# Second and third layers' output projections from fp32r halves, modulation sums in the value projections, and scores of two heads in turn

## What is computed

```python
    for i in range(DEPTH):                       # first_block: gMLP, then MLA, both with memory attention
        mix, q_mem = ...
        x = x + jnp.concatenate([mix, mem_out], axis=-1) @ w_out      # 256x1536 @ 1536x1024
        x = x + hierarchical_moe(rms_norm(x, norm2_g[i]), ...)        # 32 experts, all evaluated
...
    ada_in = jax.nn.silu(c)
    for i in range(DEPTH):                       # second_block
        mod = (ada_in @ w_ada[i] + b_ada[i]).reshape(b, 6, d)         # w_ada[i]: 1024 x 6144
        sh_m, sc_m, g_m = ...                    # modulation: shift, scale, gate
        hm = rmsnorm(x, norm_mix[i]) * (1 + sc_m) + sh_m
        y = dilated_mixer(hm, ...)  if i == 0 else forgetting_mixer(hm, ...)
        x = x + g_m * y                          # y ends in "@ w_out", 1024x1024
        hf = rmsnorm(x, norm_ffn[i]) * (1 + sc_f) + sh_f
        x = x + g_f * hierarchical_moe_2(hf, ...)                     # 16 experts, all evaluated
```

## Time and profile before

| | |
|---|---|
| three runs | 1508.47, 1515.75, 1517.82 us; median 1515.75 |
| the profiled execution | 1506.89 us; its span, first to last instruction, 1505.2 us |
| granted TensorE clock, mean over the span | 0.988 |
| busy: TensorE, VectorE, ScalarE, GpSimd | 94%, 49%, 33%, 7% |
| moved by DMA | 469.80 MB, 312 GB/s over the span |

### The profile page before, as it was taken

One profiled execution on the slowest core, in us unless ns is written; L12 is line 12 of the kernel. 1 busy time (PEld: TensorE's weight loads), 2 busy tenths in 40 slices (PEclk: granted clock), 3 DMA queues, 4 the chain that ended last, 5 costly groups with the idle time before them and its releaser, 6 DMA issues. The chain is left out here.

```text
span 1505.2 us, 23579 instructions
## 1 busy us (share of the span) xinstructions
PE 1412.2 (94%) x9085; PEld 770.8 (51%) x9090; DVE 737.2 (49%) x1659; ACT 495.8 (33%) x996; POOL 102.9 (7%) x258
## 2 busy tenths in 40 slices
PE   7999999998899899999779998899899998989998
PEld 4486433322375544333227876788655337755432
DVE  1368333221255545322227755675585346669534
ACT  3222121111226403111126656565612126661211
POOL 0000021110000001111102000200001102000110
PEclk9999999999999999999999999999999999999999
DMA  8996989999974269999997472335279997427996
GB/s 359 372 350 254 417 347 415 420 421 421 427 299 186 113 281 415 399 422 421 420 425 303 174 286 72 112 146 211 91 270 422 420 424 300 170 110 297 422 420 250
DMA packets 63400, 469.80 MB, mean 312 GB/s; under 512 B 7809, under 2 KB 15921, under 8 KB 18738
## 3 DMA queue, kind: packets, MB, share of 16 engines
q1 hardware_dynamic: 63282, 468.22, 76.7%
HBM read 465.42 MB, written 2.76 MB: 311 GB/s over the span
## 5 line engine op out<-in xcount | busy, mean ns | idle before, releaser
L1664 PE MATMUL PS<-ring,catT 128*32 128x512 f32 x3072 | 347.9, 594 | 12.3 <-issue 11.9
L826 PE MATMUL PS<-w_split,h_split 128*128 128x512 f32 x1152 | 270.0, 393 | 6.0 <-DVE w_split L911 6.0
L826 PEld LDWEIGHTS PS<-w_split,h_split 128*128 128x128 f32 x1152 | 213.6, 188 | 56.1 <-DVE w_split L911 8.5
L1664 PEld LDWEIGHTS PS<-ring,catT 128*32 128x32 f32 x3072 | 95.8, 110 | 228.2 <-issue 227.9
L911 DVE TENSOR_TENSOR w_split<-ring,w_split 128x512 fp32r<-128x512 f32 x192 | 133.5, 711 | 66.4 <-ACT w_split L859 66.1
L1687 PE MATMUL PS<-ring,row_place 128*32 128x512 f32 x1232 | 141.8, 593 | 14.0 <-issue 14.0
L859 ACT CAST w_split<-ring 128x512 fp32r<-128x512 f32 x192 | 118.0, 619 | 104.1 <-PE PS L826 103.6
L1874 ACT ACTIVATE row_place<-PS 128x256 f32<-128x256 f32 x48 | 18.5, 385 | 360.3 <-PE PS L1664 360.3
L508 PE MATMUL PS<-ring,catT 128*128 128x512 f32 x224 | 96.7, 592 | 1.0 <-PEq L1022 1.0
L1687 PEld LDWEIGHTS PS<-ring,row_place 128*32 128x32 f32 x1232 | 40.9, 110 | 104.9 <-issue 104.3
L1557 POOL COPY catT<-xsT 128x256 f32 x176 | 63.1, 402 | 395.0 <-PE PS L1664 387.4
(11 more groups left out here) (445 smaller groups left out, 1835.0 us busy)
## 6 DMA issues: line engine op xcount, KB each, us to landing
ring<-in_moe SPq DMA_DIRECT2D x269, 1024.0 KB, 13.8
ring<-in_w_ada SPq DMA_DIRECT2D x16, 3072.0 KB, 12.1
ring<-in_a_w_in SPq DMA_DIRECT2D x23, 2048.0 KB, 10.4
ring<-in_b_w_in SPq DMA_DIRECT2D x8, 2048.0 KB, 20.3
first_down<-in_moe SPq DMA_DIRECT2D x8, 1024.0 KB, 8.5
ring<-in_a_w_out SPq DMA_DIRECT2D x2, 3072.0 KB, 14.4
ring<-in_b_w_out SPq DMA_DIRECT2D x2, 3072.0 KB, 16.4
ring<-in_w_mem_kv SPq DMA_DIRECT2D x2, 2048.0 KB, 12.2
```

The source lines that it names most:

```text
L826: last = nc.tensor.matmul(PS[:, 2 * (i % 2) + t, :], hs[:, hp, k, t * P:(t + 1) * P], wk[:, (KT * i + k) % splits, wp, :], start=k == 0 an ...
L1664: last = nc.tensor.matmul(PS[lanes, 4 + i % 2, :].rearrange("p (g f) -> p g f", g=2), xf[:, i % 2, k, lanes], gate_up_weights(2 * i + q % ...
```

## The change

- `project_rows_split`, a new function, makes the output projections of the second and third layer from halves as `project_heads_split` does: 24 and 16 k tiles of six matmuls, room for four split k tiles, and the last three k tiles of the second column half taken row tile by row tile. It sums no modulation chunk. The fourth layer keeps `project_rows`.
- Of the 5 chunks that this frees, two go into the value jobs of each half of the third layer and one into those of the fourth (`sums`). Their places in the list of chunks move: 2 chunks (6 MB) leave the part ahead of the second expert stage, 3 (9 MB) the part ahead of the third. `project_heads_split` loads the silu row once the last mean is made.
- `scores1` of the dilated attention takes the two heads of a pair in turn, group by group.

```diff
 c_bin = weight_amid("b_w_in", 8, [512, 320, 512], [0, 1, 1])
 c_qup = weight("b_w_q_up", 4, [1536])
 c_kvup = weight("b_w_kv_up", 2, [2048])
-c_bout = weight_amid("b_w_out", 12, [512] * 2, [1, 0], 1)
+c_bout = weight("b_w_out", 12, [512] * 2)
 c_moe1 = experts("moe1", 32, ASIDE[1])
-c_ain2 = weight("a_w_in_2", 8, [512] * 18)
-c_aout2 = weight_amid("a_w_out_2", 8, [512] * 2, [1, 0], 2)
+c_ain2 = weight_amid("a_w_in_2", 8, [512] * 18, [0] * 8 + [1, 1] + [0] * 7 + [1], 1)
+c_aout2 = weight("a_w_out_2", 8, [512] * 2)
 c_moe2 = experts("moe2", 16, ASIDE[2])
-c_bin2 = weight("b_w_in_2", 8, [512] * 3 + [16] + [512] * 3)
+c_bin2 = weight_amid("b_w_in_2", 8, [512] * 3 + [16] + [512] * 3, [0] * 7, 1)
 c_bout2 = weight_amid("b_w_out_2", 8, [512] * 2, [1, 0], 2)
 c_moe3 = experts("moe3", 16, ASIDE[3])
+def ada_sum(c, m, row):
+    w = stream.view(ada_at[c], 6)
+    return nc.vector.tensor_tensor_reduce(w[:, m, :], w[:, m, :], row, 1.0, 0.0, ALU.mult, ALU.add, ada_out[:, 6 * c + m:6 * c + m + 1])
+def project_rows_split(srcT, k, first, gate, router, after, gain=None, shift=None, splits=4):
+    with ExitStack() as st:
...
+        HELD = 3
+        @block.sync
+        def _(sp):
...
+            stream.issue(nc, sp, first)
...
+            stream.issue(nc, sp, first + 1)
+        @block.gpsimd
+        def _(pool):
+            for j in range(k):
+                pool.wait_ge(*(h_odd if j % 2 else h_even).at(j // 2 + 1))
+                nc.gpsimd.tensor_tensor(hs[:, 1, j, :], srcT[:, j, :], hs[:, 0, j, :].bitcast(F32), ALU.subtract).then_inc(h_low.sem, 1)
+        @block.tensor
+        def _(pe):
+            def product(c, j, t, h, w):
+                return nc.tensor.matmul(PS[:, 2 * c + t, :], hs[:, h, j, t * P:(t + 1) * P], wk[:, (k * c + j) % splits, w, :],
+                                        start=j == 0 and h == 0 and w == 0, stop=j == k - 1 and h == 1)
...
+            for c in range(2):
+                held = k - HELD if c else k
+                for j in range(held):
+                    if c == 0:
+                        pe.wait_ge(*(h_odd if j % 2 else h_even).at(j // 2 + 1))
+                    pe.wait_ge(*w_high.at(k * c + j + 1))
+                    for t in range(TT):
+                        product(c, j, t, 0, 0)
+                    pe.wait_ge(*w_low.at(k * c + j + 1))
+                    for t in range(TT):
+                        product(c, j, t, 0, 1)
+                    if c == 0:
+                        pe.wait_ge(*h_low.at(j + 1))
+                    for t in range(TT):
+                        last = product(c, j, t, 1, 0)
+                        if j == k - 1 and t == 0:
+                            last.then_inc(rows_ready.sem, 1)
+                    last.then_inc(w_used.sem, 1)
+                for t in range(TT if held < k else 0):
+                    for j in range(held, k):
+                        if t == 0:
+                            pe.wait_ge(*w_low.at(k * c + j + 1))
+                        for h, w in ((0, 0), (0, 1), (1, 0)):
+                            last = product(c, j, t, h, w)
+                    last.then_inc(rows_ready.sem, 1)
...
+        @block.scalar
+        def _(act):
+            def high(c, j):
+                if j == 0:
+                    act.wait_ge(*stream.landed(first + c))
+                n = k * c + j
+                if n >= splits:
+                    act.wait_ge(*w_used.at(n - splits + 1))
+                nc.scalar.copy(wk[:, n % splits, 0, :], stream.view(first + c, k)[:, j, :]).then_inc(w_high.sem, 1)
...
+            nc.scalar.activation(stat[:, 2, 30:31], ones_f[:, 0:1], ACT.Sqrt)
+            for j in range(0, k, 2):
+                nc.scalar.copy(hs[:, 0, j, :], srcT[:, j, :]).then_inc(h_even.sem, 1)
+                high(0, j)
+                high(0, j + 1)
+            for j in range(k):
+                high(1, j)
...
+        @block.vector
+        def _(dve):
+            def low(c, j):
+                n = k * c + j
+                dve.wait_ge(*w_high.at(n + 1))
+                nc.vector.tensor_tensor(wk[:, n % splits, 1, :], stream.view(first + c, k)[:, j, :], wk[:, n % splits, 0, :].bitcast(F32),
+                                        ALU.subtract).then_inc(w_low.sem, 1)
+                if j == k - 1:
+                    dve.wait_ge(*w_low.at(n + 1))
+                    nc.vector.sem_inc(chunk_used, 1)
...
+            for j in range(0, k, 2):
+                nc.vector.tensor_copy(hs[:, 0, j + 1, :], srcT[:, j + 1, :]).then_inc(h_odd.sem, 1)
+                low(0, j)
+                low(0, j + 1)
+                if j == 4:
+                    if gate is not None:
+                        dve.wait_ge(*gate_made.at(1))
+                        nc.vector.tensor_copy(gain, PS[:, 6:8, :].rearrange("p b n -> p (b n)")).then_inc(gate_made.sem, 1)
+                        dve.wait_ge(*gate_made.at(2))
+                    after()
+            for j in range(k):
+                low(1, j)
+                if j == splits - 1:
+                    add(0)
+                if j == splits:
+                    add(1)
+            add(2)
+            add(3)
...
+        silu_row = catT[:, 8:12, :].rearrange("p k n -> p (k n)")
...
         def chunk(i):
-            return first + i + (1 if side is not None and i >= 3 else 0)
+            return first + i + (1 if side is not None and i >= 3 else 0) + (1 if len(sums) > 1 and i == len(jobs) - 1 else 0)
...
+            stream.issue(nc, sp, chunk(turns[-1] + 1))
+            sp.wait_ge(*mean_ready.at(len(turns)))
+            load_silu_row(silu_row)
             if load_last is not None:
-                stream.issue(nc, sp, chunk(turns[-1] + 1))
                 sp.wait_ge(*turned.at(2 * len(turns)))
                 load_last(sp)
-            stream.issue(nc, sp, chunk(len(jobs)))
+            stream.issue(nc, sp, chunk(len(jobs) - 1) + 2)
...
+            def ada(c, ms):
+                if ms[0] == 0:
+                    dve.wait_ge(*stream.landed(ada_at[c]))
+                for m in ms:
+                    last = ada_sum(c, m, silu_row)
+                if ms[-1] == 5:
+                    dlink(last)
+                    nc.vector.sem_inc(chunk_used, 1)
             for i, job in enumerate(jobs):
+                if i == len(jobs) - 3 + (len(sums) == 1):
+                    dve.wait_ge(*silu_loaded.at(16))
+                if len(sums) > 1 and i >= len(jobs) - 2:
+                    ada(sums[0], range(2, 4)) if i == len(jobs) - 2 else ada(sums[1], range(0, 6))
+                if len(sums) == 1 and i == len(jobs) - 1:
+                    ada(sums[0], range(2, 6))
...
+                if len(sums) > 1 and i == len(jobs) - 2:
+                    ada(sums[0], range(4, 6))
+                if i == len(jobs) - 3 + (len(sums) == 1):
+                    ada(sums[0], range(0, 1))
                 low(i + 1, range(splits + 3, KT))
+                if i == len(jobs) - 3 + (len(sums) == 1):
+                    ada(sums[0], range(1, 2))
                 low(i + 2, range(0, splits))
...
-            def scores1(i, y, parts):
-
-                if parts[0] == 0 and i >= 1:
-                    pe.wait_ge(*logits_ready[1].at(2 * (i - 1) + y + 1))
-                for s in parts:
+            def scores1(i, s):
+                if s == 0 and i >= 1:
+                    pe.wait_ge(*logits_ready[1].at(2 * i))
+                for y in range(2):
                     last = score_one(i, 1, y, s)
-                if parts[-1] == 2:
-                    last.then_inc(scores_ready[1].sem, 1)
+                    if s == 2:
+                        last.then_inc(scores_ready[1].sem, 1)
...
                 if i < n:
-                    scores1(i, 0, (0, 1))
+                    scores1(i, 0)
                 if i:
                     turn(i - 1, 2)
                     turn(i - 1, 3)
                 if i < n:
-                    scores1(i, 0, (2,))
-                    scores1(i, 1, (0,))
+                    scores1(i, 1)
                 if i:
                     turn(i - 1, 4)
                     turn(i - 1, 5)
                 if i < n:
-                    scores1(i, 1, (1, 2))
+                    scores1(i, 2)
...
-    project_rows(catT, 12, c_bout, [512] * 2, add_rows(None), ada=[1, 0], ada_last=1, after=lambda: modulation(0, (0, 48), (0, 1)), router=1)
+    project_rows_split(catT, 12, c_bout, None, 1, lambda: modulation(0, (0, 48), (0, 1)))
...
-                project_heads_split(hT, c_ain2 + half * 9, jobs, rows=z_rows, load_last=load_two_biases,
+                project_heads_split(hT, c_ain2 + half * 11, jobs, rows=z_rows, load_last=load_two_biases, sums=(8 + 2 * half, 9 + 2 * half),
...
-    project_rows(catT, 8, c_aout2, [512] * 2, add_rows(grow[:]), ada=[1, 0], ada_last=2, after=lambda: modulation(1, (0, 24), (0,)), router=2, gate=mod[:, 0, 16:24], shift=mod[:, 0, 24:32])
```

(6 more changed lines are left out.)

41 lines of the change are left out of this document (added).

## The result

| kernel | runs | median us | ratio to before, 95% interval |
|---|---|---|---|
| before | 4 | 1515.62 | |
| changed | 4 | 1548.90 (1546.55 to 1555.79) | 1.0214 (1.0169 to 1.0259) |

The change makes the kernel 33 us slower, 2.1% (1.7 to 2.6%). The profiled execution is the slowest of the four: 1555.79 us, with a span of 1554.1.

What follows compares the result with a forecast made beforehand. TensorE, busy 1412.2 of 1505.2 us, was taken as the bound. Terms -5.2 - 3.8 - 2.2 + 10.8 + 4.8 + 1.5 = +5.9 us, added to 1512.1, gave 1518 us, range 1500 to 1529.

Steps and rivals of the forecast that it cites:

- The step that failed: Third layer's dilated attention: bias loads queued behind up to ten expert pieces are needed two passes later, so cost nothing.
- part 2: Value projections of the third and fourth layers: summing five chunks there costs 10.8 us and 4.8 us.
- The sums: End of value jobs: sums delay VectorE's last copy 5.4 us in each third-layer half, 3.4 us in the fourth layer.
- part 5: TensorE pauses before the attentions and second projection: half clock behind them costs 1.5 us, bounds 0 to 6.4.
- The silu row: Fourth layer's last value job: VectorE waits 4 us, TensorE's low half comes 1.6 us late; 4.8 us with the sums.
- Projections and scores: Projections from halves gain 5.2 us in layer 2 and 3.8 in layer 3; alternate scores in dilated attention gain 2.2.
- part 3: Modulation weights leaving the loads ahead of the second and third expert stages gain nothing; tail waits stay at 12 us.
- (A): Rival: VectorE's tail at the value jobs' end is not on the path; 1502 to 1504 us, chance 0.12.
- (D): Rival: fp32r matmuls of the projections wait for their weights, so halves gain nothing; 1527 us, chance 0.04.
- (B): Rival: freed DMA time removes up to 12 us of waits in the second expert stage's tail; 1506 us, chance 0.08.
- (C): Rival: every pause brings a half-clock stretch, up to 8 us beyond the 1.5 counted; 1526 us, chance 0.13.

Runs made afterwards that it cites:

- e3: Changed kernel, but only two more chunks are issued at the end of each half's value jobs, the rest behind the bias rows; 1527.35 us, ratio 1.0086.
- e5: e3 with the fourth layer's silu row loaded as soon as the last mean is made; 1523.03 us, ratio 1.0032.
- e8: e5 without the five chunks' sums in the value jobs, a memset of six columns for each; 1505.07 us, ratio 0.9933.
- e1: The kernel before with only the alternate scores (scores1) added; 1510.35 us, ratio 0.9965.

## Why the prediction was wrong

Forecast +5.9 us on the profiled execution, 1518 us in all, range 1500 to 1529; measured 1548.9, +33 us. It had given a chance of 0.09 to slower by over 1%.

- **The step that failed** stands in part 2: of the bias loads in SyncE's queue, "most of them issued before the attention begins, and they are needed two passes of its loop later. Nothing." Three things are wrong in it. What counts is when the bytes ahead have landed, not when they are issued. The third pair's row is needed one pass after its issue, since its buffer is the first pair's: issued from 921.2, asked for at 939.13 - 8.29 = 930.8. I had costed it as two passes. And it looked at the second half alone (and there at the ten pieces without the 6 MB of `a_w_out_2`), where the first has a burst of 14 MB too. Shown by e3: 21.5 us by the medians, 19.4 by the ratios, the waits of 8.3 and 7.5 us and the half clock behind them.
- **The sums.** Place, order, pause and size were right: 5.0 and 5.5 us more pause before the dilated attentions, against 5.4 forecast, and for all five chunks 15.0 us by the ratios and 15.1 on the traces (18.0 by the medians) against 10.8 + 3.4 + 1.5 = 15.7. "TensorE: Matmul & The Clock Gate" of the Trainium skill (Why this matters for your kernels) advises against idle gaps between bursts of matmuls; by its rule, with every pause paid, the estimate would have come to 10.8 + 3.4 + 6.4 = 20.6 us. The traces agree that a low clock follows such pauses (in e5 0.81 over the first 22 us of the last attention, behind 4.87 us; before 1.00, behind 1.03), but the sum of what it costs is nearer to the working. One reason given in part 5 does not hold, though: that the pause of 2.67 us has full-rate matmuls behind it. In the changed kernel the same pause is followed by the same 66 records in 16.83 us instead of 15.24, with no edit there (16.8 in five of the twelve traces, 15.2 in seven):

```profile
967.69 16.83 PE L979 MATMUL PS<-w_split,h_split 128*128 128x512 f32 x66 [2.67 <-DVE w_split L1064]
```

- **The silu row.** The mechanism was right and the size short: 9.9 us in all for the fourth layer's value jobs against 4.8 (6.4 in the jobs, 3.5 in the pause). VectorE had it at 1354.7, 13 us after its issue, behind 2.1 MB of key_bias and the 2.1 MB of b_w_out, as the working had it (12). But VectorE asked for it at 1348.3, 6.7 us after the issue and not 8. The lead that TensorE lived on was as forecast, 6.42 - 3.57 = 2.9 us against 4 - 1.6 = 2.4; the half clock behind the wait (2.5 us), which the working left out, has the rest. e5 took the 5.9 us of it back.
- **Projections and scores** came out right in the sum, in part by luck: 11.2 us of gain forecast (5.2, 3.8, 2.2), and e8, where all else is taken away, is 10.6 us below before (6 to 14). Of these the projections have 4.7 and 4.4 us at their ends and 3.8 and 3.5 up to the experts' rows; the scores have 2.2 on the trace and 4.8 in e1's runs. What e1 has beyond the trace stays open.
- **DMA (part 3)** was right for the expert stages (67.32 of 80.5 us busy at the end of the second one, 68.01 of 80 before), and wrong in taking the stages for all that the ring matters to: room taken by modulation chunks came back as a burst in front of a small load.
- **Rivals.** (A) and (D) are excluded by the pauses and by the rows at L624, (B) by the expert stage. (C), the halved clock, is at work on top of the pauses, though it is not a mechanism of its own: e3, which leaves the pauses in, has 29.0 and 30.4 us for the scores, so most of the low clock there came with the wait for the bias.

From the changed kernel down to e8, by the medians: bias rows 21.5, silu row 4.3, sums 18.0, which is 43.8 us; by the ratios 19.4, 8.2 and 15.0, which is 42.6. The rest of the change is 10.6 us (10.2) below before. That these close to 33 us is no check, since each kernel of the row is the last one with one edit more; the intervals of the single steps are 4 to 7 us to either side. The term that the forecast put at nothing, the bias rows, is two thirds or more of what it missed.

## What to carry to other kernels

Chunks that only pass through a ring still take its room: what they push out is issued later and in a burst, and every small load issued behind the burst waits for all of its bytes. So for each load in a queue, count the bytes ahead that have not landed when it is issued, and set that against the time of its first use. Here that alone gives about 929; the row came ten us later, since the issuing queue was held and the rows moved at less than half the rate, so a forecast by bytes is the least that it takes. Remove delays together before pricing one: with the bias wait in place the sums seemed to cost 7 to 9 us, without it 15 to 18.

## What the runs showed of the hardware

Six loads of 128 KB each are issued in 3.7 us when little is ahead of them (e3) and in 11.2 us behind a burst of 14 MB (the changed kernel): SyncE's own queue is held too, not only the landing. And the granted clock differs between executions where the code does not: the same stretch of the second layer ran at 0.51 (1.2 GHz) in one profile and at 1.00 in another, 5 us of work apart, which is more than half of the spread of 9 us that the four runs of the changed kernel show. Over the twelve traces the time up to the second layer's output projection, where no instruction of TensorE was edited, goes from 518.8 to 526.9 us: the four above 522 have 14 to 17 us at the half clock, the other eight 3 to 10.
